# First scores of the second attention inside its value projection, its weight preparation in quarters; stick-breaking's first value slab fetched ahead of the key slab

## The chip, the cores and the metric

The kernel runs on one core of one Trainium2 chip. The metric is the device time of one execution in microseconds. The kernel before took 2044.36 us as the median of three runs (2042.57 to 2048.69). The execution from which the trace comes took 2052.48 us; all rows below come from that one.

## The reference, cut to what matters

Two transformer blocks run one after the other on one sequence of 512 tokens, width 1024, in float32. The first is feed-forward, a mixer, feed-forward. The second is retention followed by stick-breaking attention. Two places matter here.

```python
# block 1, the mixer: 12 heads in three dilation groups; one softmax over all three groups' keys comes out of the mixture
q, k, v = heads(u @ w_in)                      # u = rms_norm(h)
q, k = apply_partial_rope(q), apply_partial_rope(k)
s = einsum(q, k) * HEAD_DIM ** -0.5; s = where(allowed, s, -inf)   # per group
p = exp(s - max(s)); o = einsum(p, v) / sum(p); lse = max(s) + log(sum(p))
alpha = softmax(stack(lses)); y = sum(alpha * stack(outs))
# block 2, stick-breaking: 8 heads, keys and values from kv = rms_norm(h, kv_norm) @ w_kv
z = einsum(q, k) / sqrt(128)                   # q = (rms_norm(h, sb_norm_pre) @ sb_w_in)[:, :1024]
log_not = where(causal, log_sigmoid(-z), 0)
weights = exp(log_sigmoid(z) + reverse_cumsum(log_not) - log_not)
out = einsum(weights, v)
```

## The kernel before, in words

The order of the work is written out by hand, once per engine, with semaphores between the engines. Every weight comes as a slab of 128x2048 numbers (1 MB) into one of two slots (`raw`, `RING = 2`). ScalarE copies a slab to its rounded part `w_hi` (`prep`, L349) once the slot's former slab is used up, VectorE computes the rest `w_lo = raw - w_hi` (L728), and TensorE multiplies in three passes (high by high, low by high, high by low: L1339, L1340, L1341) into the banks of `acc` or `att` (four each). SyncE fetches slab n (`fetch`, L253) once slab n-2 is prepared. `prep` is called one slab ahead of its use, at fixed places in the order of ScalarE and VectorE.

The mixer has two attentions, `attend(0)` and `attend(1)`, of two head columns each. Each takes eight units (a token residue times a head). A unit k on TensorE is `scores(k)` (nine matmuls on 64 rows), `turn(k)` (six fp32 matmuls at L1499 that transpose the probabilities and scale them by `diag`) and the mix with the values (six matmuls at L1520). In the loop TensorE does `scores(k + 2)`, `turn(k + 1)`, mix k. On VectorE a unit is: scale and mask the scores (L888, L890), their maximum (L893), the low part of the transposed probabilities of unit k + 1 (L915, L917), a reciprocal (L908), and the sum of the mix (L932). On ScalarE: copy the transposed probabilities (L474, L476), exp (L452), `diag` (L458). Between units, `between()` prepares one whole slab: on ScalarE at k = 5, on VectorE at k = 6.

Ahead of each attention stands the value projection `values(x, strided, ...)`: four blocks of 24 matmuls, one per residue, whose stationary operand is every fourth token of `x`. In the second attention the last key rotation (`rotate_last`, L1443 and L1444) stands behind block 1, and the first two scores (`first_scores`) stand behind block 3, directly ahead of `attend(1)`. In the first attention the first scores stand one whole strided value projection ahead of `attend(0)`.

Stick-breaking begins in `sb_start`. TensorE makes the first keys from slab `sb_kq[0]` and the first values from slab `sb_v[0]`, interleaved over the input chunks, then eight fp32 matmuls for a mean (L1725, shown as 16), then the query, again from `sb_kq[0]`, then the turned norms (L1399). The third slab, `sb_g[0]`, goes into the slot of `sb_kq[0]`; its `prep` stands last in `sb_start` on both engines, behind `split_values` (L444 and L789). Then `sb_body` starts: four score matmul groups, then `pair()` with slab `sb_g[0]`, then the cumulative sums (L1686, L1687) that need `sp_lo`. For these VectorE goes through L1250, L1255, L1257, L1263 and L738, and ScalarE through L669, L671 and L354.

Of the kernel before, what the change touches and what calls it, by code (L numbers as in the profile page):

```python
# [30 lines left out]
SLAB = 16 * BLK  # L31
RING = 2
# [56 lines left out]
def block_kernel(nc, dram, out):  # L89
    with ExitStack() as ctx:  # L90
# [129 lines left out]
        w_ready = sem("w_ready")  # L220
        seg_done = sem("seg_done")
# [24 lines left out]
        def _(sp):  # L246
# [48 lines left out]
            for j in range(2):  # L295
                fetch(dram["ret_out"][RET_HEADS - 1, j])
            fetch(dram["sb_kq"][0])
            fetch(dram["sb_v"][0])
# [39 lines left out]
        def _(act):  # L338
# [3 lines left out]
            def prep(cols=SLAB):  # L342


                slot = n.k % RING
                act.wait_ge(raw_landed[slot], n.landed())
                if s.k:
                    act.wait_ge(seg_done, s.at())
                nc.scalar.activation(w_hi[:, slot, 0:cols], raw[:, slot, 0:cols], ACT.Copy).then_inc(w_hi_ready, 1)  # L349
                n.next()  # L350

# [118 lines left out]
            def attend(a, between=None):  # L470
# [10 lines left out]
                for k in range(UNITS):  # L481
                    if k == UNITS - 3 and between is not None:
                        between()
                    if k + 1 < UNITS:
                        stage(k + 1)
                    if k + 2 < UNITS:
                        exps(k + 2)
                        normalizer(k + 2)

# [29 lines left out]
            attend(0, prep)  # L519
# [5 lines left out]
            mix_values(2, 1)  # L525
            exps(1)
            normalizer(1)
            attend(1, prep)
# [125 lines left out]
            def sb_start():  # L654

                split_kq(0)
                std_of()
# [4 lines left out]
                prep()  # L662
# [56 lines left out]
        def _(dve):  # L719
            n, s, u, b = Count(), Count(), Count(), Count()  # L720
            fn, hi, step, sq, prob, mix, op, squared = (Count() for _ in range(8))
# [3 lines left out]
            def prep(cols=SLAB):  # L725
# [3 lines left out]
                n.next()  # L729

# [179 lines left out]
            def attend(a, between=None):  # L910
# [10 lines left out]
                for k in range(UNITS):  # L921
                    if k == UNITS - 2 and between is not None:
                        between()
# [4 lines left out]
                    if k + 2 < UNITS:  # L928
# [4 lines left out]
                                            ALU.add).then_inc(acc_free, 2)  # L933
                u.next(2 * UNITS)
# [57 lines left out]
            attend(0, prep)  # L992
# [6 lines left out]
            normalizer(0)  # L999
            mix_values(2, 1)  # L1000
            normalizer(1)
            attend(1, prep)
# [217 lines left out]
            def sb_start():  # L1220

                split_kq(0)
                rstd_of()
# [6 lines left out]
                prep()  # L1230
# [83 lines left out]
        def _(pe):  # L1314
# [237 lines left out]
            values(x, strided, {1: rotate_last, 3: first_scores})  # L1552
# [153 lines left out]
            def sb_start():  # L1706

                w, wv = slab(), slab()
# [156 lines left out]
```

## Time and profile before

| | |
|---|---|
| three timed runs, median | 2044.36 us |
| profiled execution, its time | 2052.48 us |
| its span, first to last instruction | 2050.7 us |
| TensorE matmul busy | 1978.7 us (96%) |
| VectorE busy | 1189.1 us (58%) |
| ScalarE busy | 700.0 us (34%) |
| mean granted TensorE clock | 0.979 of full |

TensorE is the busy engine nearly everywhere, so a time is found where TensorE stands idle or where its granted clock is below full. In the timeline each row is one instruction or a run of equal ones: start, duration, line, operation, and in square brackets the idle time before it with the instruction that ended it. Durations of matmuls overlap, so the step from one start to the next says what one costs.

### The profile page before, as it was taken

The numbers are of one execution on the slowest core, as the hardware profiler recorded it, in microseconds if no ns is written. First come the engines' busy times: TensorE is split into PE (matmuls) and PEld (weight loads), VectorE is DVE, ScalarE is ACT, GpSimd is POOL, SyncE is SP. The second block draws the span as 40 slices with busy tenths as digits, with TensorE's granted clock in tenths as the row PEclk, the third lists the DMA queues.
The fourth block names the chain that finished last, engine by engine and source line by source line (L and its number), as shares of the span: only waits on it lengthen the run. The fifth ranks groups of instructions, "written<-read, shape, count | busy, mean of one in ns | idle before, by whom it ended". The sixth has DMA issues, their size and how long they took to land.

```text
span 2050.7 us, 24191 instructions
## 1 busy us (share of the span) xinstructions
PE 1978.7 (96%) x9308; PEld 1668.2 (81%) x9308; DVE 1189.1 (58%) x1418; ACT 700.0 (34%) x744; POOL 11.3 (1%) x19
## 2 busy tenths in 40 slices
PE   7999999999999999999999999999997999999995
PEld 5888888889887788888888888888885788888884
DVE  5343355675545566434455658584859665555557
ACT  4222232334224333222232233232324544444443
POOL 0000000000000000000000000000000000000000
PEclk9999999999969999999999999999998999999998
DMA  4222223320202222222223322221212122222211
GB/s 174 92 92 102 83 85 99 121 78 11 78 0 78 92 103 97 89 101 102 84 80 108 129 82 84 81 95 69 102 62 82 42 83 70 75 81 82 82 62 41
DMA packets 27413, 171.77 MB, mean 84 GB/s; under 512 B 3184, under 2 KB 3200, under 8 KB 10464
## 3 DMA queue, kind: packets, MB, share of 16 engines
q1 hardware_dynamic: 25344, 165.95, 23.0%
q0 software_dynamic: 864, 2.99, 0.4%
q10 hardware_dynamic: 1152, 2.10, 0.3%
q8 instruction: 37, 0.61, 0.1%
q14 instruction: 16, 0.13, 0.0%
HBM read 168.93 MB, written 2.10 MB: 83 GB/s over the span
## 4 chain that ended last, share of the span: by engine, by line
PE 90%; DVE 6%; ACT 2%; issue 1%; DMA 0%; DVEq 0%; ACTq 0%; POOLq 0%
PE acc L1339 27%; PE acc L1340 26%; PE acc L1341 26%; PE att L1339 2%; PE att L1341 2%; PE att L1340 2%; PE acc L1499 1%; DVE w_lo L728 1%; ACT w_hi L349 1%; DVE rstd L769 1%; PE acc L1520 1%; PE att L1687 1%; PE att L1686 1%; DVE tmp L1187 0%; PE att L1725 0%
## 5 line engine op out<-in xcount | busy, mean ns | idle before, releaser
L1339 PE MATMUL acc<-x_hi,w_hi 128*128 128x512 f32 x1408 | 555.5, 395 | 20.0 <-DVE w_lo L728 17.9
L1340 PE MATMUL acc<-x_lo,w_hi 128*128 128x512 f32 x1408 | 549.9, 391 | 0.0
L1341 PE MATMUL acc<-x_hi,w_lo 128*128 128x512 f32 x1408 | 549.9, 391 | 0.0
L728 DVE TENSOR_TENSOR w_lo<-raw,w_hi 128x2048 fp32r<-128x2048 f32 (+1 forms) x168 | 383.0, 2280 | 140.0 <-ACT w_hi L349 135.7
L349 ACT ACTIVATE w_hi<-raw 128x2048 fp32r<-128x2048 f32 (+1 forms) x168 | 318.8, 1898 | 106.4 <-PE acc L1341 103.0
L1339 PEld LDWEIGHTS acc<-x_hi,w_hi 128*128 128x128 f32 x1408 | 265.4, 188 | 78.6 <-DVE w_lo L728 18.0
L1340 PEld LDWEIGHTS acc<-x_lo,w_hi 128*128 128x128 f32 x1408 | 265.6, 189 | 56.9 <-issue 2.4
L1341 PEld LDWEIGHTS acc<-x_hi,w_lo 128*128 128x128 f32 x1408 | 265.5, 189 | 55.9
L1339 PE MATMUL acc<-g_hi,w_hi 128*128 128x512 f32 x352 | 136.9, 389 | 0.0
L1340 PE MATMUL acc<-g_lo,w_hi 128*128 128x512 f32 x352 | 136.9, 389 | 0.0
L1341 PE MATMUL acc<-g_hi,w_lo 128*128 128x512 f32 x352 | 136.9, 389 | 0.0
L382 ACT ACTIVATE tmp<-tmp 128x512 f32<-128x512 f32 x44 | 27.8, 632 | 293.3 <-DVE tmp L801 293.3
L801 DVE TENSOR_TENSOR tmp<-acc,rstd 128x512 f32<-128x512 f32 x44 | 30.4, 691 | 159.3 <-PE acc L1341 159.2
L1339 PE MATMUL acc<-w_hi,x_hi 128*128 128x512 f32 (+1 forms) x224 | 84.6, 378 | 1.1 <-DVE w_lo L728 1.1
L1340 PE MATMUL acc<-w_lo,x_hi 128*128 128x512 f32 (+1 forms) x224 | 84.5, 377 | 0.0
L1341 PE MATMUL acc<-w_hi,x_lo 128*128 128x512 f32 (+1 forms) x224 | 84.4, 377 | 0.0
L1341 PEld LDWEIGHTS acc<-g_hi,w_lo 128*128 128x128 f32 x352 | 66.1, 188 | 13.8
L1340 PEld LDWEIGHTS acc<-g_lo,w_hi 128*128 128x128 f32 x352 | 66.1, 188 | 13.7
L1339 PEld LDWEIGHTS acc<-g_hi,w_hi 128*128 128x128 f32 x352 | 66.1, 188 | 13.6
L1339 PE MATMUL acc<-w_hi,kv_hi 128*128 128x256 f32 x224 | 63.7, 284 | 0.0
L1340 PE MATMUL acc<-w_lo,kv_hi 128*128 128x256 f32 x224 | 63.4, 283 | 0.0
L1341 PE MATMUL acc<-w_hi,kv_lo 128*128 128x256 f32 x224 | 63.4, 283 | 0.0
(277 smaller groups left out, 2922.8 us busy)
## 6 DMA issues: line engine op xcount, KB each, us to landing
raw<-in_ffn_up SPq DMA_DIRECT2D x44, 1024.0 KB, 4.7
raw<-in_ret_head SPq DMA_DIRECT2D x24, 1024.0 KB, 4.7
raw<-in_ffn_down SPq DMA_DIRECT2D x32, 704.0 KB, 4.0
raw<-in_mix_gate SPq DMA_DIRECT2D x8, 1024.0 KB, 4.8
raw<-in_ret_out SPq DMA_DIRECT2D x8, 1024.0 KB, 4.7
raw<-in_sb_kq SPq DMA_DIRECT2D x8, 1024.0 KB, 4.7
raw<-in_sb_v SPq DMA_DIRECT2D x8, 1024.0 KB, 4.7
raw<-in_sb_g SPq DMA_DIRECT2D x8, 1024.0 KB, 4.7
```

The source lines that it names most:

```text
L349: nc.scalar.activation(w_hi[:, slot, 0:cols], raw[:, slot, 0:cols], ACT.Copy).then_inc(w_hi_ready, 1)
L382: nc.scalar.activation(t(j), t(j), ACT.Silu).then_inc(fn_ready, 1)
L728: tt(w_lo[:, slot, 0:cols], raw[:, slot, 0:cols], w_hi[:, slot, 0:cols].bitcast(F32), ALU.subtract).then_inc(w_ready, 1)
L769: nc.vector.reciprocal(dst[:], t(std)).then_inc(att_free, 1 + skip)
L801: tt(t(j), acc[:, u.k % BANKS, :], rstd[:], ALU.mult).then_inc(acc_free, 1)
L1339: mm(dst, still[0], move[0], start=first, stop=False)
L1340: mm(dst, still[0], move[1], start=False, stop=False)
L1341: return mm(dst, still[1], move[0], start=False, stop=last)
L1499: last = mm(dst[i // TB][:, P * (i % TB):P * (i % TB) + P], tmp[:, at:at + P], diag[:, k % 2, :], start=True, stop=True)
L1520: last = mm(dst, va[:, k_blk, value_slot(g, head)].rearrange("p s d -> p (s d)"), turned_probs[:, k % 2, i].rearrange("p s q -> p (s q)"), ...
L1686: mm(dst[:, P * (k - m):TRI[m]], still[:], sp_hi[:, cols], start=k == m, stop=False)
L1687: ins = mm(dst[:, P * (k - m):TRI[m]], still[:], sp_lo[:, cols], start=False, stop=k == TB - 1)
```

## The change

Three edits, and what goes with them.

1. In the second attention TensorE's rotation moves behind block 0 of the value projection, and the first two scores move behind block 1, ahead of blocks 2 and 3. ScalarE and VectorE do `exps`/`normalizer` of both units before they take over values 2 and 3.
2. In both attentions the slab is prepared in four parts of 512 columns, at the end of the iterations k = 1 to 4, on ScalarE behind `normalizer(k + 2)` and on VectorE behind the sum of mix k. A new semaphore `w_part_ready` passes the first three parts on.
3. SyncE fetches `sb_v[0]` ahead of `sb_kq[0]`; TensorE takes the two in that order. So `sb_g[0]` goes into the slot of `sb_v[0]`, and its `prep` moves on ScalarE and VectorE from the end of `sb_start` to directly behind `split_kq(0)`.

```diff
+PARTS = 4
+PART = SLAB // PARTS
@@ sync
+            fetch(dram["sb_v"][0])
             fetch(dram["sb_kq"][0])
-            fetch(dram["sb_v"][0])
             fetch(dram["sb_g"][0])
@@ scalar
+            def prep_part(i):
+                slot, cols = n.k % RING, slice(PART * i, PART * (i + 1))
+                if i == 0:
+                    act.wait_ge(raw_landed[slot], n.landed())
+                    act.wait_ge(seg_done, s.at())
+                nc.scalar.activation(w_hi[:, slot, cols], raw[:, slot, cols], ACT.Copy).then_inc(
+                    w_hi_ready if i == PARTS - 1 else w_part_ready, 1)
+                if i == PARTS - 1:
+                    n.next()
@@ scalar, attend
                 for k in range(UNITS):
-                    if k == UNITS - 3 and between is not None:
-                        between()
                     if k + 1 < UNITS:
                         stage(k + 1)
                     if k + 2 < UNITS:
                         exps(k + 2)
                         normalizer(k + 2)
+                    if 1 <= k <= PARTS:
+                        prep_part(k - 1)
@@ scalar, second attention
             exps(0)
             normalizer(0)
-            mix_values(2, 1)
             exps(1)
             normalizer(1)
-            attend(1, prep)
+            mix_values(2, 1)
+            attend(1)
@@ scalar, sb_start
                 split_kq(0)
+                prep(seg=2)
                 std_of()
...
-                prep()
@@ vector
+            def prep_part(i):
+                slot, cols = n.k % RING, slice(PART * i, PART * (i + 1))
+                if i < PARTS - 1:
+                    dve.wait_ge(w_part_ready, part.next())
+                else:
+                    dve.wait_ge(w_hi_ready, n.at(1))
+                ins = tt(w_lo[:, slot, cols], raw[:, slot, cols], w_hi[:, slot, cols].bitcast(F32), ALU.subtract)
...
@@ vector, attend
-                    if k == UNITS - 2 and between is not None:
-                        between()
...
                     nc.vector.tensor_reduce(o_unit[:, k, :], ...).then_inc(acc_free, 2)
+                    if 1 <= k <= PARTS:
+                        prep_part(k - 1)
@@ tensor
-            values(x, strided, {1: rotate_last, 3: first_scores})
+            values(x, strided, {0: rotate_last, 1: first_scores})
@@ tensor, sb_start
-                w, wv = slab(), slab()
+                wv, w = slab(), slab()
```

VectorE inside `attend(0)`, one iteration of the loop (k = 1) before, from the scaled scores to the next ones:

```order
L888 SCALAR_TENSOR_TENSOR tmp<-att,band 128x512 [waits att_full]
L890 SCALAR_TENSOR_TENSOR tmp<-att,classes 128x256
L893 TENSOR_REDUCE neg_max<-tmp 128x1 [waits att_free]
L915 TENSOR_TENSOR stage<-acc,stage 128x4x128 [waits hi_ready]
L917 TENSOR_TENSOR stage<-acc,stage 128x2x128 [waits hi_ready]
L908 RECIPROCAL rden<-den 128x1 [waits prob_ready]
L932 TENSOR_REDUCE tmp<-acc 128x128 [waits mixed]
L888 SCALAR_TENSOR_TENSOR tmp<-att,band 128x512 [waits att_full]
```

The same iteration in the changed kernel, whose line numbers are higher by 24 to 26:

```order
L914 SCALAR_TENSOR_TENSOR tmp<-att,band 128x512 [waits att_full]
L916 SCALAR_TENSOR_TENSOR tmp<-att,classes 128x256
L919 TENSOR_REDUCE neg_max<-tmp 128x1 [waits att_free]
L941 TENSOR_TENSOR stage<-acc,stage 128x4x128 [waits hi_ready]
L943 TENSOR_TENSOR stage<-acc,stage 128x2x128 [waits hi_ready]
L934 RECIPROCAL rden<-den 128x1 [waits prob_ready]
L956 TENSOR_REDUCE tmp<-acc 128x128 [waits mixed]
L752 TENSOR_TENSOR w_lo<-raw,w_hi 128x512 [waits w_part_ready]
L914 SCALAR_TENSOR_TENSOR tmp<-att,band 128x512 [waits att_full]
```

A quarter of the slab now stands between two units, and it waits for ScalarE's quarter of the same iteration.

TensorE at the end of value block 1 of the second attention before (the blocks are L1339 to L1341 on `x`, the rotation is L1443 and L1444):

```order
L1341 MATMUL acc<-w_hi,x_lo 128x256
L1443 MATMUL att<-stage,rot_r 128x512
L1444 MATMUL att<-stage,rot_r 128x512
L1339 MATMUL acc<-w_hi,x_hi 128x256
L1340 MATMUL acc<-w_lo,x_hi 128x256
```

The same place in the changed kernel:

```order
L1367 MATMUL acc<-w_hi,x_lo 128x256
L1365 MATMUL att<-qk_hi 128x512
L1366 MATMUL att<-qk_lo,qk_hi 128x512
L1367 MATMUL att<-qk_hi,qk_lo 128x512
L1365 MATMUL att<-qk_hi 128x128
```

The scores (`att<-qk`) now stand where the rotation stood, and blocks 2 and 3 follow them; the rotation stands one block earlier.

VectorE from the first key split of stick-breaking to its first scaled scores before (L728 is the preparation of slab `sb_g[0]`):

```order
L738 TENSOR_TENSOR skq_lo<-acc,skq_hi 128x512 [waits hi_ready]
L769 RECIPROCAL rstd<-tmp 128x512 [waits fn_ready]
L738 TENSOR_TENSOR skq_lo<-acc,skq_hi 128x512 [waits hi_ready,att_free]
L782 COPY r_tok<-att 128x4 [waits att_full]
L1227 TENSOR_SCALAR z_scale<-r_tok 128x4 [waits att_free]
L789 SCALAR_TENSOR_TENSOR sv_lo<-acc,r_tok,sv_hi 128x256 [waits hi_ready,dve_step]
L789 SCALAR_TENSOR_TENSOR sv_lo<-acc,r_tok,sv_hi 128x256
L789 SCALAR_TENSOR_TENSOR sv_lo<-acc,r_tok,sv_hi 128x256 [waits hi_ready]
L789 SCALAR_TENSOR_TENSOR sv_lo<-acc,r_tok,sv_hi 128x256
L728 TENSOR_TENSOR w_lo<-raw,w_hi 128x2048 [waits w_hi_ready]
L1250 SCALAR_TENSOR_TENSOR tmp<-att,z_scale,rstd 128x512 [waits att_full,op_ready]
```

The same stretch in the changed kernel:

```order
L764 TENSOR_TENSOR skq_lo<-acc,skq_hi 128x512 [waits hi_ready]
L742 TENSOR_TENSOR w_lo<-raw,w_hi 128x2048 [waits w_hi_ready]
L795 RECIPROCAL rstd<-tmp 128x512 [waits fn_ready]
L764 TENSOR_TENSOR skq_lo<-acc,skq_hi 128x512 [waits hi_ready,att_free]
L808 COPY r_tok<-att 128x4 [waits att_full]
L1254 TENSOR_SCALAR z_scale<-r_tok 128x4 [waits att_free]
L815 SCALAR_TENSOR_TENSOR sv_lo<-acc,r_tok,sv_hi 128x256 [waits hi_ready,dve_step]
L815 SCALAR_TENSOR_TENSOR sv_lo<-acc,r_tok,sv_hi 128x256
L815 SCALAR_TENSOR_TENSOR sv_lo<-acc,r_tok,sv_hi 128x256 [waits hi_ready]
L815 SCALAR_TENSOR_TENSOR sv_lo<-acc,r_tok,sv_hi 128x256
L1276 SCALAR_TENSOR_TENSOR tmp<-att,z_scale,rstd 128x512 [waits att_full,op_ready]
```

The preparation of `sb_g[0]` moved from behind the value splits to ahead of the reciprocal.

## Rows read from the trace of the kernel before

**Rows 1.** Page, part 2: granted TensorE clock in 40 slices of 51.3 us.
```profile
PEclk9999999999969999999999999999998999999998
```

**Rows 2.** Timeline, TensorE, first attention: start, us, line, operation, [idle before].
```profile
481.60 1.50 PE L1499 MATMUL acc<-tmp 128*128 128x128 f32 x12
...
505.68 0.63 PE L1339 MATMUL att<-qk_hi 64*128 64x512 f32 x1
...
507.96 1.60 PE L1499 MATMUL acc<-tmp 128*128 128x128 f32 x12
...
511.83 1.60 PE L1499 MATMUL acc<-tmp 128*128 128x128 f32 x12 [1.55 <-ACT tmp L458]
...
514.87 0.98 PE L1520 MATMUL acc<-stage,va 128*128 128x256 f32 x6 [0.73 <-DVE stage L917]
```

**Rows 3.** Timeline, TensorE, second attention.
```profile
564.72 0.28 PE L1339 MATMUL acc<-w_hi,x_hi 128*128 128x256 f32 x1
...
579.09 0.41 PE L1341 MATMUL att<-qk_hi,qk_lo 64*128 64x128 f32 x1
582.85 2.93 PE L1499 MATMUL acc<-tmp 128*128 128x128 f32 x12 [3.35 <-ACT tmp L458]
...
618.62 0.62 PE L1339 MATMUL att<-qk_hi 64*128 64x512 f32 x1
...
627.81 0.98 PE L1520 MATMUL acc<-stage,va 128*128 128x256 f32 x6 [0.73 <-DVE stage L917]
```

**Rows 4.** Stretches: length, busy and instructions per engine, granted clock, DMA share, GB/s.
```profile
40.00:60.00 20.00, 20.00 (x90) 16.57 (x89) 7.73 (x8) 5.51 (x5) 0.00 (x0) 1.00 0.34 123
...
459.00:460.00 1.00, 1.00 (x6) 1.00 (x5) 0.97 (x2) 0.00 (x0) 0.00 (x0) 0.50 1.00 418
462.00:463.00 1.00, 1.00 (x6) 1.00 (x6) 0.02 (x1) 0.95 (x2) 0.00 (x0) 1.00 0.63 262
584.00:588.00 4.00, 4.00 (x17) 3.51 (x15) 1.66 (x5) 1.71 (x5) 0.00 (x0) 0.50 0.00 0
```

**Rows 5.** Timeline, TensorE, start of stick-breaking.
```profile
1620.63 0.27 PE L1341 MATMUL att<-skq_hi,skq_lo 128*128 128x128 f32 x1
1624.56 0.50 PE L1339 MATMUL acc<-x_hi,w_hi 128*128 128x512 f32 x1 [3.66 <-DVE w_lo L728]
...
1637.19 0.41 PE L1686 MATMUL att<-sp_hi,tri_r 128*128 128x512 f32 x1
```

**Rows 6.** Timeline, VectorE, start of stick-breaking.
```profile
1619.75 1.66 DVE L789 SCALAR_TENSOR_TENSOR sv_lo<-acc,r_tok,sv_hi 128x256 fp32r<-128x256 f32 x4 [0.77 <-ACT sv_hi L444]
...
1624.42 1.92 DVE L1250 SCALAR_TENSOR_TENSOR tmp<-att,z_scale,rstd 128x512 f32<-128x512 f32 x4
...
1635.56 1.49 DVE L738 TENSOR_TENSOR sp_lo<-tmp,sp_hi 128x1280 fp32r<-128x1280 f32 x1 [1.34 <-ACT sp_hi L354]
```

**Rows 7.** Timeline, VectorE: first scaled scores of the second attention.
```profile
578.37 0.69 DVE L888 SCALAR_TENSOR_TENSOR tmp<-att,band 128x512 f32<-128x512 f32 x1 [9.73 <-PE att L1341]
```

**Rows 8.** Timeline, ScalarE: second `diag` of the second attention, and start of stick-breaking.
```profile
584.66 0.40 ACT L458 ACTIVATE tmp<-ident,rden 128x128 f32<-128x128 f32 x1 [0.23 <-DVE rden L908]
...
1611.84 0.69 ACT L363 ACTIVATE tmp<-att,eps 128x512 f32<-128x512 f32 x1 [7.70 <-PE att L1725]
```

**Rows 9.** Timeline, VectorE, small slab preparation and two units of the first attention.
```profile
457.50 0.68 DVE L728 TENSOR_TENSOR w_lo<-raw,w_hi 128x512 fp32r<-128x512 f32 x1
458.10 0.68 DVE L888 SCALAR_TENSOR_TENSOR tmp<-att,band 128x512 f32<-128x512 f32 x1
...
503.54 0.69 DVE L888 SCALAR_TENSOR_TENSOR tmp<-att,band 128x512 f32<-128x512 f32 x1 [0.92 <-PE att L1341]
...
508.07 0.69 DVE L888 SCALAR_TENSOR_TENSOR tmp<-att,band 128x512 f32<-128x512 f32 x1 [0.92 <-PE att L1341]
```

**Rows 10.** Timeline, ScalarE: the small slab preparation, and the whole one in the first attention.
```profile
455.02 0.64 ACT L349 ACTIVATE w_hi<-raw 128x512 fp32r<-128x512 f32 x1
...
507.15 1.89 ACT L349 ACTIVATE w_hi<-raw 128x2048 fp32r<-128x2048 f32 x1
```

More of the change, by code:

```diff
@@ L220, in block_kernel @@
         w_ready = sem("w_ready")
+        w_part_ready = sem("w_part_ready")
         seg_done = sem("seg_done")
@@ L340, in _, with prep @@
             val, turn, inv = Count(), Count(), Count()
-            def prep(cols=SLAB):
+            def prep(cols=SLAB, seg=0):
                 slot = n.k % RING
@@ L347, in prep @@
                 if s.k:
-                    act.wait_ge(seg_done, s.at())
+                    act.wait_ge(seg_done, s.at(seg))
                 nc.scalar.activation(w_hi[:, slot, 0:cols], raw[:, slot, 0:cols], ACT.Copy).then_inc(w_hi_ready, 1)
                 n.next()
+            def prep_part(i):
[7 more added lines that the diff above has]
+                    n.next()
             def split_val(dst, src):
@@ L468, in gather, with attend @@
                                      ACT.Copy).then_inc(hi_ready, 1)
-            def attend(a, between=None):
+            def attend(a):
                 def stage(k):
@@ L518, in _ @@
             mix_values(1, 1)
-            attend(0, prep)
+            attend(0)
             qk(True)
@@ L720, in _ @@
             n, s, u, b = Count(), Count(), Count(), Count()
-            fn, hi, step, sq, prob, mix, op, squared = (Count() for _ in range(8))
+            fn, hi, step, sq, prob, mix, op, squared, part = (Count() for _ in range(9))
             tt = nc.vector.tensor_tensor
@@ L729, in prep @@
                 n.next()
+            def prep_part(i):
[5 more added lines that the diff above has]
+                ins = tt(w_lo[:, slot, cols], raw[:, slot, cols], w_hi[:, slot, cols].bitcast(F32), ALU.subtract)
+                if i == PARTS - 1:
+                    ins.then_inc(w_ready, 1)
+                    n.next()
             def link(ins):
@@ L908, in normalizer, with attend @@
                 nc.vector.reciprocal(rden[:, k:k + 1], den[:, k:k + 1]).then_inc(rden_ready, 1)
-            def attend(a, between=None):
+            def attend(a):
                 def low_probs(k):
@@ L991, in _ @@
             mix_values(1, 1)
-            attend(0, prep)
+            attend(0)
             qk(True)
@@ L999, in _ @@
             normalizer(0)
+            normalizer(1)
             mix_values(2, 1)
-            normalizer(1)
-            attend(1, prep)
+            attend(1)
             gather(1)
@@ L1222, in sb_start @@
                 split_kq(0)
+                prep()
                 rstd_of()
@@ L1229, in sb_start @@
                     split_values(lambda k: sv_lo[:, k:k + 1, :], lambda k: sv_hi[:, k:k + 1, :], o, 0, whole_row)
-                prep()
             def sb_out(first, last):
```

## The prediction

> **What bounds the kernel now.** I read the page first. TensorE is busy nearly everywhere, and its granted clock has one deep hole: slices 12 and 13 of 40 read 9 and 6 [rows 1], and the timeline shows that the hole is the second attention. The timeline of TensorE there and the same place in the first attention are the two stretches to lay side by side. Both do the same instructions. In the first, `turn(0)` starts at 481.60, `scores(7)` at 505.68 and the last mix at 514.87 [rows 2]. In the second the first scores end at 579.50, TensorE stands idle for 3.35 us until `diag` is there, `turn(0)` starts at 582.85, `scores(7)` at 618.62, the last mix at 627.81 [rows 3]. From `turn(0)` to `scores(7)` that is 24.08 us against 35.77, and from there to the last mix 9.19 in both. The granted clock says why: 0.50, which is 1.2 GHz, from 584 to 588 [rows 4], and the twelve matmuls of a turn take 2.93 us where they take 1.50 in the first [rows 2, 3].
>
> Then the timeline at the start of stick-breaking. TensorE ends its scores at 1620.90 and starts the pair with slab `sb_g[0]` at 1624.56, after 3.66 us of idle time ended by `w_lo` [rows 5]. VectorE starts its scaled scores at 1624.42, behind that same `w_lo` [rows 6].
>
> **Edit 1, the scores inside the value projection.** No matmul is added or taken out. Blocks 2 and 3 now stand between the scores and `turn(0)`. Block 2 starts at 564.72 and the scores end at 579.50 [rows 3]; two score groups take at most 2.3 us each (505.68 to 507.96) [rows 2], so the two blocks give at least 10.2 us of cover. What must fit under them is the chain from the first scaled scores to the second `diag`. It started at 578.37 [rows 7] and ended at 585.06 [rows 8], so 6.7 us; it started 1.1 us before the end of the scores, so it ends 5.6 us behind that, and over 4 us are spare. VectorE now takes over values 0 and 1 in front of it, and four such takeovers take 1.66 us [rows 6]. If the cover fell away, at most the 3.35 us would come back. The takeover of values 2 and 3 slides behind the start of `turn(0)`, exactly where the first attention has it, and there it holds nobody up. Gain: 3.35 us of idle time.
>
> The larger part is the clock. It fell around the idle time and stayed at 1.2 GHz for most of the attention. Entered at 2.4 GHz, the second attention should take what the first takes: 35.77 - 24.08 = 11.69 us less.
>
> One rule has to be held against that. The rows show a fall with no idle time at all: at 459 TensorE was fully busy at 0.50, just behind the first attention's first scores, and at 462 it was back at 1.00, both times inside the strided value blocks [rows 4]. The changed kernel puts just these scores ahead of just such blocks, so I expect such a fall here too. It costs nothing there: six matmuls stand in a microsecond at either level [rows 4]. The Trainium skill, "TensorE: Matmul & The Clock Gate", Part 1, says that "the default state is throttled, and activity releases the throttle", and puts the low state down to idleness. By that rule closing the gap is enough; by the row at 459 it isn't, and the entry into the attention must find the clock raised again. The rule alone gives the sum below, the row without the recovery at 462 gives rival A.
>
> **Edit 2, the preparation in quarters.** It removes one ScalarE copy (1.89 us) and one VectorE subtraction per attention and adds four of each. Two ends. On the good side, the last mix waits 0.73 us for `stage` behind the whole subtraction [rows 2, 3]; a good part of that wait is the ordinary chain turn, copy, subtract, so I book 0.2 us. On the bad side stands a loop through two engines. VectorE starts the scaled scores of a unit at 503.54 [rows 9]; ScalarE is through with `diag` and free at 507.15 [rows 10]: 3.61 us. Behind it now come ScalarE's quarter, 0.64 us [rows 10], and VectorE's quarter, which waits for it and holds up the next scaled scores by 0.60 us (457.50 to 458.10) [rows 9]. The sum is 4.85 us, and a unit on TensorE has 508.07 - 503.54 = 4.53 [rows 9]. So each of four iterations makes VectorE 0.32 us later, 1.28 us in all. The slack: `turn(6)` starts 4.42 us behind its scaled scores (503.54 to 507.96), while `turn(7)`, which waits for nothing else, starts 3.76 behind (508.07 to 511.83) [rows 2, 9]. So 0.66 us are hidden at first, but `turn(7)` has no slack, and gets the whole 1.28 us. Queued behind the waiting quarter on VectorE are the scaled scores, for which ScalarE's exp and then TensorE's turn wait. Net per attention 1.28 - 0.2 = 1.1 us lost, 2.2 for both. Bounds: 0.7 gained each (the whole wait) to 1.3 lost each. I take the lost end, since its terms are rows. The slab itself was not waited for here, so having it earlier brings nothing; SyncE's next fetch comes about 10 us earlier, into an idle queue.
>
> **Edit 3, the value slab first.** `sb_g[0]`'s preparation moves into a hole: ScalarE was idle for 7.70 us before 1611.84 [rows 8], and VectorE's next instruction waits for that copy. Into this fit 1.9 us and then at most four times 0.60. Both slabs are needed for the first matmul either way, so their exchange costs nothing. VectorE's scaled scores then start at 1619.75 + 1.66 = 1621.41 in place of 1624.42: 3.01 us earlier [rows 6]. The pair could start at 1620.90, 3.66 us earlier, and at full clock. What is late next is `sp_lo`: it ended at 1637.05 and the cumulative sums started at 1637.19, without idle time [rows 5, 6]. So the gain is the smaller one, 3.0 us, if ScalarE's part of the chain shifts with it, and the pair, 48 matmuls where 90 go in 20 us [rows 4], takes 10.7 us and ends at 1631.6, leaving some 2.6 us idle before the sums at about 1634.2. Bounds: 0 to 3.7 us. SyncE's fetch of `sb_v[1]` comes some 15 us earlier, with nothing behind it.
>
> **The sum**, against the profiled execution: 2052.48 - 3.35 - 11.69 + 2.2 - 3.0 = 2036.6 us. The median is 8.1 us below that execution, and this is the weakest place of the forecast. If the difference is in every profiled run, the median of the changed kernel is 2044.4 - 15.8 = 2028.5. If it is clock that the profiled run lost and the timed runs did not, it is 2036.6. The three timed runs lie 6.1 us apart, about half of the 11.7, which looks like clock. I take the middle, 2032.5. The Trainium skill, same page and part, says of the cold start that "it's run-variable"; the spread agrees with it, but no row here shows a second execution.
>
> **Rivals.**
> A. The clock is low on entry all the same, because it falls behind the moved scores and isn't raised before `turn(0)`. Then only the idle time goes, the quarters are hidden in the slow units, and the sum is 2044.4 - 3.35 - 3.0 + 1.1 = 2039.1. For it: the fall at 459. Against it: at 462 it had been raised, under the same blocks, which go on for 10 us or more here.
> B. The new gaps cost clock. `turn(7)` now waits 1.55 + 1.28 = 2.8 us in both attentions [rows 2], and stick-breaking gets the 2.6 us. What a short fall costs before dense matmuls is in the rows: 1624.56 to 1637.19 is 12.6 us [rows 5], 1.9 more than 10.7. Three times that: 2032.5 + 5.7 = 2038.2. For it: lengths of gaps near 3.35. Against it: the gap of 1.55 us fell nowhere.
> C. Slower: the quarters open waits inside the first attention's units, the clock falls there before `turn(1)`, and both attentions run at 1.2 GHz. The first then pays the 11.7 us that only the second paid, the second gets only its 3.35 back, the quarters cost nothing at that pace: 2044.4 + 11.7 - 3.35 - 3.0 = 2049.7. It decides only if the fall comes in the first units; the first wait that I compute comes at `turn(6)`, which speaks against it.
> D. Nothing moves, since the timed runs never lost the clock that the trace lost and the quarters eat the rest: 2044.
>
> **Chances.** Forecast 0.69, A 0.11, B 0.12, C 0.05, D 0.03. A change of 0.3% (6.1 us) is about what a measurement can tell, so faster means below 2038.2. Of the forecast nearly all, of A four tenths and of B half lie below: 0.80 faster. The same 0.14, slower 0.06. The range must hold 2028.5 with the quarters hidden and the whole 3.7 us (2025) and reach through B and A: 2025 to 2041.
>
> **What would show it.** In the changed kernel's trace: `turn(0)` of the second attention directly behind value block 3, a turn there in about 1.5 us, 24 us from it to `scores(7)`, and the clock at 1.00; `turn(7)` in the first attention 31.5 us behind `turn(0)` instead of 30.2, with its wait grown from 1.55 to 2.8; in stick-breaking no wait of the pair, and one of about 2.6 us ahead of the sums, for `sp_lo`. I am wrong if the second attention reads 0.50 again, or if `turn(7)` is not later.

## The result: 8 to 10 us faster, and a forecast that was 8 us too low

The changed kernel takes 2040.51 us (median of 16 runs, 2038.75 to 2042.11), the kernel before 2048.45 us (16 runs, 2042.14 to 2058.50). The ratio is 0.9959, interval 0.9946 to 0.9972. On a second occasion it was 2039.97 against 2049.89 us, ratio 0.9955 (0.9937 to 0.9974). The time lies in the forecast range, near its upper end, and the kernel is faster by more than 0.3%. The value of 2032.5 us was 8.0 us too low. Three executions in the whole record stand far outside the others (2494.82 and 8305.98 us of the kernel before, 5971.66 us of `e7_tails_filled`); they are left out of the ranges below, and without them the medians beside them would be 0.1 to 0.3 us lower.

The profiled execution of the changed kernel took 2041.25 us (span 2039.4), that of before 2052.48 (span 2050.7). The deep hole in the granted clock is gone. The page of the changed kernel, part 2, answers to [rows 1]:

```profile
PEclk9999999999999999999999999999998999999998
```

The timeline of TensorE in the changed kernel answers to [rows 2] and [rows 3]. The first three rows are of the first attention, the others of the second: `turn(0)`, the first row of `scores(7)`, `turn(7)` and the last mix, then the gather behind it.

```profile
484.50 1.50 PE L1525 MATMUL acc<-tmp 128*128 128x128 f32 x12
...
511.19 2.12 PE L1525 MATMUL acc<-tmp 128*128 128x128 f32 x12 [0.26 <-ACT tmp L472]
516.05 2.92 PE L1525 MATMUL acc<-tmp 128*128 128x128 f32 x12 [1.46 <-ACT tmp L472]
...
584.61 1.50 PE L1525 MATMUL acc<-tmp 128*128 128x128 f32 x12
...
608.68 0.63 PE L1365 MATMUL att<-qk_hi 64*128 64x512 f32 x1
...
616.15 1.60 PE L1525 MATMUL acc<-tmp 128*128 128x128 f32 x12 [2.54 <-ACT tmp L472]
...
619.04 0.98 PE L1546 MATMUL acc<-stage,va 128*128 128x256 f32 x6 [0.58 <-DVE stage L943]
620.61 1.98 PE L1500 MATMUL att<-tmp,fold 128*128 128x512 f32 x4 [0.59 <-DVE tmp L956]
```

`turn(0)` of the second attention has no wait in brackets any more, and from it to `scores(7)` are 24.07 us (584.61 to 608.68) in place of 35.77. ScalarE had both `diag` long ready:

```profile
576.22 0.40 ACT L472 ACTIVATE tmp<-ident,rden 128x128 f32<-128x128 f32 x1 [0.95 <-DVE rden L934]
...
577.77 0.40 ACT L472 ACTIVATE tmp<-ident,rden 128x128 f32<-128x128 f32 x1 [0.23 <-DVE rden L934]
```

`turn(0)` waits only for the first of them, which was ready at 576.62, 8.0 us before TensorE starts at 584.61. Even the second, which `turn(1)` reads at 588.32, was there 6.4 us before `turn(0)`. In the first attention `turn(7)` starts 31.55 us behind `turn(0)` (484.50 to 516.05), 1.32 later than before. It takes 2.92 us, the time of a turn at 1.2 GHz; before it took 1.60 [rows 2].

The granted clock of these stretches in the changed kernel (length, busy and instructions of PE, PEld, DVE, ACT and POOL, then PEclk, DMA share, GB/s), to be laid beside [rows 4]:

```profile
508.00:511.00 3.00, 2.93 (x15) 2.62 (x13) 2.80 (x7) 1.70 (x5) 0.00 (x0) 1.00 0.00 0
511.00:512.00 1.00, 0.81 (x7) 0.82 (x8) 0.36 (x2) 0.65 (x2) 0.00 (x0) 1.00 0.00 0
512.00:515.00 3.00, 2.59 (x14) 2.29 (x12) 2.96 (x6) 1.65 (x3) 0.00 (x0) 0.52 0.41 134
515.00:518.00 3.00, 1.95 (x9) 1.96 (x10) 0.73 (x3) 0.76 (x3) 0.00 (x0) 0.50 0.51 216
...
574.00:576.00 2.00, 2.00 (x10) 2.00 (x10) 1.97 (x4) 1.03 (x2) 0.00 (x0) 0.50 0.00 0
584.00:588.00 4.00, 4.00 (x25) 3.88 (x24) 1.80 (x4) 1.71 (x4) 0.00 (x0) 1.00 0.00 0
```

There is a fall behind the moved scores (574 to 576), and it is over before the attention begins (584 to 588 reads 1.00 where [rows 4] read 0.50). There is also a new one at the end of the first attention, low for 6.8 us. In the second profiled execution of the same kernel, `after_again`, it is 3.4 us long, and the first attention takes 34.44 us there and not 35.40.

At the start of stick-breaking the timeline of TensorE answers to [rows 5], and that of VectorE to [rows 6]:

```profile
1609.17 0.50 PE L1365 MATMUL att<-skq_hi 128*128 128x512 f32 x1 [0.70 <-DVE skq_lo L764]
...
1624.41 0.51 PE L1712 MATMUL att<-sp_hi,tri_r 128*128 128x512 f32 x1 [2.15 <-DVE sp_lo L764]
...
1628.80 0.45 PE L1365 MATMUL acc<-kv_hi,w_hi 128*128 128x512 f32 x1
```

```profile
1610.16 1.66 DVE L815 SCALAR_TENSOR_TENSOR sv_lo<-acc,r_tok,sv_hi 128x256 fp32r<-128x256 f32 x4 [0.77 <-ACT sv_hi L458]
1611.74 1.92 DVE L1276 SCALAR_TENSOR_TENSOR tmp<-att,z_scale,rstd 128x512 f32<-128x512 f32 x4
...
1622.87 1.49 DVE L764 TENSOR_TENSOR sp_lo<-tmp,sp_hi 128x1280 fp32r<-128x1280 f32 x1 [1.34 <-ACT sp_hi L368]
```

The pair no longer waits (no row of it has brackets), VectorE's scaled scores follow the splits at once, and the sums wait 2.15 us for `sp_lo`. Then the sums run slowly: their windows show the clock down exactly there.

```profile
1621.00:1624.00 3.00, 1.26 (x6) 0.72 (x4) 1.66 (x2) 2.42 (x2) 0.00 (x0) 1.00 0.50 208
1624.00:1628.00 4.00, 3.58 (x15) 3.44 (x15) 2.24 (x4) 2.64 (x4) 0.00 (x0) 0.60 0.00 0
```

The whole difference between the two profiled executions, from the starts of the same rows in both timelines:

| stretch | before | after | difference | forecast |
|---|---|---|---|---|
| start to first `turn(0)` | 481.60 | 484.50 | +2.90 | 0 |
| first attention, `turn(0)` to last mix | 33.27 | 35.40 | +2.13 | +1.1 |
| last mix to second `turn(0)` | 67.98 | 64.71 | -3.27 | -3.35 |
| second attention, `turn(0)` to gather | 46.52 | 36.00 | -10.52 | -10.6 |
| gather to first scores of stick-breaking | 989.39 | 988.56 | -0.83 | 0 |
| these scores to the sums | 18.43 | 15.24 | -3.19 | -3.0 |
| sums to the next key slab | 2.74 | 4.39 | +1.65 | 0 |
| from there to the end | 410.77 | 410.60 | -0.17 | 0 |

The differences add up to the 11.3 us between the spans. These are two single executions; the kernel before varies by 16 us from run to run, so its row for the second attention stands for its slower runs.

### The profile page after: what moved, and what is told of

Its sections match the earlier page's. It is cut to its first block, busy times and chain, and to the rows that moved or that the text cites. A ratio compares the mean times of both kernels' runs of the same rounds, so it can differ in the third digit from the quotient of the medians.

```text
span 2039.4 us, 24203 instructions
## 1 busy us (share of the span) xinstructions
PE 1968.8 (97%) x9308; PEld 1660.7 (81%) x9308; DVE 1189.2 (58%) x1424; ACT 701.1 (34%) x750; POOL 11.3 (1%) x19
## 4 chain that ended last, share of the span: by engine, by line
PE 88%; DVE 7%; ACT 3%; issue 1%; DMA 0%; DVEq 0%; ACTq 0%
PE acc L1365 26%; PE acc L1367 26%; PE acc L1366 26%; PE att L1365 2%; PE att L1367 2%; PE att L1366 2%; ACT w_hi L352 1%; DVE w_lo L742 1%; DVE rstd L795 1%; PE att L1713 1%; PE att L1712 1%; ACT tmp L466 1%; DVE neg_max L919 0%; PE acc L1525 0%; DMA h<-in_x 0%
## 5 line engine op out<-in xcount | busy, mean ns | idle before, releaser
L742 DVE TENSOR_TENSOR w_lo<-raw,w_hi 128x2048 fp32r<-128x2048 f32 (+1 forms) x166 | 378.4, 2280 | 141.3 <-ACT w_hi L352 137.2
```

The source lines that it names most:

```text
L742: tt(w_lo[:, slot, 0:cols], raw[:, slot, 0:cols], w_hi[:, slot, 0:cols].bitcast(F32), ALU.subtract).then_inc(w_ready, 1)
```

## The experiments

In all of them the pattern of the clock is read from the granted clock in windows of 1 us. "Low for 34.1 us" means the sum of the time at 1.2 GHz in one such stretch.

### Each edit alone, and two together

The scores alone, `e1_scores_only`:

```
-            values(x, strided, {1: rotate_last, 3: first_scores})
+            values(x, strided, {0: rotate_last, 1: first_scores})
```

(and the order of `mix_values`, `exps(1)` and `normalizer(1)` that goes with it).

> The kernel before with edit 1 alone (rotation and first scores inside the value projection; whole slab preparation as before). Theory (the wait ahead of the second attention costs the clock of that attention): the 3.35 us of idle time go, turn(0) to scores(7) takes 24.1 us as in the first attention at a granted clock of 1.00, and since runs of the kernel before lose different amounts of clock there, the median falls by 3.35 plus 4 to 8 us, that is by 7 to 11 us, and the runs lie closer together than those of before. Rival (only the idle time counts, the clock is lost somewhere in the attention anyway): 3.4 us less and the spread stays.

Measured: 2038.82 us (2037.20 to 2040.77) against 2049.95 of the kernel before, ratio 0.9941 (0.9920 to 0.9962).

The quarters alone, `e2_quarters_only`: both `prep_part` functions and their calls, the scores and the slab as before.

> The kernel before with edit 2 alone (slab preparation of both attentions in quarters). Theory (the loop VectorE scores, ScalarE exp and diag, ScalarE quarter, VectorE quarter is 0.3 us longer than a unit): turn(6) and turn(7) of the first attention come 0.3 and 1.3 us later, the longer wait ahead of turn(7) can cost the clock there, and the time rises by 1 to 3 us (the second attention, at half clock, hides its quarters). Rival (quarters fit between the units, the whole slab was in the way of the last mix): 0.2 to 0.7 us less per attention.

Measured: 2046.97 us (2045.73 to 2047.96), ratio 0.9986 (0.9973 to 0.9998).

The slab of stick-breaking alone, `e3_slab_only`:

```
-                w, wv = slab(), slab()
+                wv, w = slab(), slab()
```

(with the exchanged fetches and the two moved `prep` calls).

> The kernel before with edit 3 alone (first value slab ahead of the key slab, its successor prepared in the hole). Theory: the pair starts 3.7 us earlier, the cumulative sums 3.0 us earlier, a wait of 2.2 us for sp_lo opens ahead of them; 2 to 3.2 us less, according to the clock after that wait. Rival (the new wait costs a clock stretch as long as the old one and cancels the gain): 0 to 1.5 us less.

Measured: 2049.88 us (2042.26 to 2055.32), ratio 0.9991 (0.9973 to 1.0009). That is 0.1 us less than before; the 2 to 3.2 us of the theory did not come, and the number is that of the rival.

Scores and slab without the quarters, `e4_no_quarters`:

> The changed kernel without edit 2 (edits 1 and 3 alone). Theory: turn(7) waits 1.55 us in both attentions, no clock is lost at the end of the first, and the time is 2 to 4 us below that of the changed kernel, 2036.5 to 2038.5. Rival (the quarters are free): the same as the changed kernel, 2040.5.

Measured: 2037.78 us (2036.96 to 2038.30), ratio 0.9936 (0.9915 to 0.9957).

What follows: edit 1 brings 11.1 us, more than the whole change. Edit 3 on top of it brings 1.0 us (2038.82 to 2037.78). The quarters take back 2.7 us (2037.78 to 2040.51, on two occasions; 2.2 us against the 2039.97 of the other occasion). That the quarters alone are not slower but 3 us faster than before (2046.97 against 2049.95) does not fit this sum. The timeline of that kernel shows the idle time ahead of the second attention whole, and a slow `turn(0)`, but the next turn (591.34, 1.60 us) is fast again, and its windows show why:

```profile
586.03 2.93 PE L1525 MATMUL acc<-tmp 128*128 128x128 f32 x12 [3.35 <-ACT tmp L472]
```

```profile
582.00:590.00 8.00, 4.65 (x19) 4.18 (x20) 5.58 (x12) 4.34 (x10) 0.00 (x0) 0.57 0.00 0
590.00:594.00 4.00, 4.00 (x26) 3.76 (x26) 2.52 (x5) 1.38 (x3) 0.00 (x0) 1.00 0.02 4
```

Here the clock was low for 6.8 us, about half of it the gap itself. In the kernel before it was low for 34.1 us around the same gap. These windows are of the kernel before:

```profile
590.00:600.00 10.00, 10.00 (x41) 9.16 (x41) 5.44 (x12) 4.19 (x9) 0.00 (x0) 0.50 0.00 0
600.00:610.00 10.00, 10.00 (x38) 9.00 (x38) 4.27 (x10) 2.70 (x6) 0.00 (x0) 0.50 0.00 0
610.00:614.00 4.00, 4.00 (x19) 3.78 (x19) 2.85 (x7) 1.89 (x4) 0.00 (x0) 0.50 0.00 0
615.00:619.00 4.00, 4.00 (x26) 3.76 (x26) 2.49 (x4) 1.35 (x3) 0.00 (x0) 1.00 0.00 0
```

So the length of the slow stretch is not fixed by the gap. Two kernels test that.

### Is it the gap, and what sets how long the clock stays down?

`e6_gap_filled` is the kernel before with 14 matmuls in the gap, whose result goes into a free bank and is read by nobody:

```
+            pe.wait_ge(acc_free, u.at(1))
+            for i in range(14):
+                mm(acc[:, u.k % BANKS, :], x_hi[:, i % DC, 0:P], x_hi[:, i % DC, :], start=True, stop=True)
             attend(1)
```

> The kernel before with 14 matmuls of 512 columns (3.2 us) into a free bank between its first scores and turn(0) of the second attention; their result is overwritten, nothing is left out. Order and waits stay. Theory (the idle 3.35 us make the clock fall): the attention runs at 1.00, turn(0) to scores(7) takes 24.1 us, the runs lie close together, and the median falls by 6 to 9 us although no wait is shorter. Rival (the clock falls because of the 64-row scores ahead of the attention, idle or not): the attention still reads 0.50 in part and the median stays near that of before.

Measured: 2043.04 us (2039.63 to 2045.19), ratio 0.9972 (0.9957 to 0.9987). The timeline shows the filler where the idle time was, and turns of 1.60 us behind it:

```profile
581.48 3.47 PE L1556 MATMUL acc<-x_hi 128*128 128x512 f32 x14
584.90 1.60 PE L1500 MATMUL acc<-tmp 128*128 128x128 f32 x12
```

```profile
582.00:586.00 4.00, 4.00 (x22) 3.17 (x22) 2.77 (x6) 2.58 (x6) 0.00 (x0) 1.00 0.00 0
586.00:590.00 4.00, 4.00 (x25) 3.77 (x24) 2.81 (x8) 1.74 (x6) 0.00 (x0) 1.00 0.02 4
```

`turn(0)` starts at the same distance from the scores as before, so nothing but the clock has changed, and the kernel is about 6.9 us faster (2049.92 to 2043.04). So the loss of clock in the second attention hangs on the idle gap: the scores ahead of it are the same, and in the profiled execution with the gap filled the clock does not fall behind them. Value blocks in the gap, as in edit 1, are better still, since they also give back the gap itself: from the filled gap to edit 1 alone are another 4.2 us (2043.04 to 2038.82), 3.3 of them idle time. The Trainium skill, "TensorE: Matmul & The Clock Gate", Part 1, puts the low state down to idleness; this run agrees with it. The fall at 459 us, with TensorE fully busy [rows 4], does not.

`e8_shift` leaves the gap alone and puts six such matmuls, 1.36 us of work, ahead of the second attention's queries and keys, 65 us before the gap:

```
             units_done = u.k + BANKS
+            pe.wait_ge(acc_free, u.at(1))
+            for i in range(6):
+                mm(acc[:, u.k % BANKS, :], x_hi[:, i % DC, 0:P], x_hi[:, i % DC, :], start=True, stop=True)
             qk(True)
```

> The kernel before with 6 matmuls of 512 columns (1.36 us) between attend(0) and the next projection; everything behind comes 1.36 us later, nothing else moves. Quarters alone made the runs of the kernel before lie close together (2045.7 to 2048.0) though the gap ahead of the second attention was still there. Theory (how long the clock stays low in the second attention depends on when, counted from the start of the kernel, the gap falls, and the quarters only moved it by 1.2 us): with the shift the slow runs over 2050 vanish too, the runs lie within 3 us, and the median is at or below that of before minus 1 us in spite of 1.36 us more work. Rival (the quarters themselves helped the clock recover): the runs spread over 10 us as those of before, and the median rises by 1.4 us.

Measured: 2043.60 us (2041.81 to 2048.47), ratio 0.9972 (0.9954 to 0.9989). With more work and the gap untouched it is about 6.3 us faster than before. All 12 runs have a mean granted clock of 0.985 to 0.988, which only 16 of 66 runs of the kernel before reach; one of the 12 (2048.47 us) lies outside the 3 us that the theory gave them. The timeline and the windows show the gap and a short fall:

```profile
586.11 2.93 PE L1500 MATMUL acc<-tmp 128*128 128x128 f32 x12 [3.35 <-ACT tmp L459]
```

```profile
582.00:590.00 8.00, 4.65 (x19) 4.21 (x19) 5.66 (x12) 4.34 (x10) 0.00 (x0) 0.57 0.00 0
590.00:594.00 4.00, 4.00 (x26) 3.76 (x26) 2.49 (x4) 1.35 (x3) 0.00 (x0) 1.00 0.01 4
```

The two profiled executions alone would not show this: that of `e8_shift` has the gap 3.26 us later than that of before, of which only 1.36 are the filler, and the rest lies ahead of the first attention. When the clock falls differs too. The first row is of the kernel before, the second of `e8_shift`:

```profile
580.00:581.00 1.00, 0.00 (x0) 0.00 (x0) 1.00 (x3) 0.59 (x1) 0.00 (x0) 0.87 0.00 0
582.00:583.00 1.00, 0.76 (x4) 0.58 (x3) 0.97 (x3) 0.00 (x0) 0.00 (x0) 0.84 0.00 0
```

A mean of 0.87 over one microsecond puts the fall before at 580.7, which is 1.2 us into the idle time. The 0.84 puts that of `e8_shift` at 582.7, and its idle time begins at 582.76, so this fall comes with the end of the scores and can't be put down to the gap behind them. In `e2_quarters_only` it is the same (0.85 in that microsecond, idle from 582.68).

What follows: filling the gap takes the low stretch away, and moving the same gap in time changes how long the clock stays down (6.8 or 34.1 us in the profiled executions). By what rule the place decides isn't shown. The spread of the kernel before goes with the clock. Over 66 of its timed runs, those taken beside the experiments, the time follows the mean granted clock of the run:

| mean clock of the run | runs | time, us | median |
|---|---|---|---|
| 0.984 to 0.988 | 24 | 2041.86 to 2047.90 | 2045.4 |
| 0.980 to 0.983 | 17 | 2048.40 to 2052.91 | 2049.8 |
| 0.976 to 0.979 | 25 | 2052.62 to 2058.47 | 2054.6 |

The changed kernel's 16 runs span 3.4 us. That these differences of clock all lie in the second attention isn't shown, since timed runs have no trace; the kernels without the gap, `e1`, `e4` and `e6`, span 1.3 to 5.6 us.

### The quarters

`e5_vector_later` is the changed kernel with VectorE's quarter one iteration later, so that ScalarE has long finished it:

```
-                    if 1 <= k <= PARTS:
-                        prep_part(k - 1)
+                    if 2 <= k <= PARTS + 1:
+                        prep_part(k - 2)
```

> The changed kernel with VectorE's quarter one iteration later than ScalarE's (k = 2 to 5), so that it no longer waits for the quarter of its own iteration. Theory (the loop of two engines is 0.3 us too long because VectorE waits there): without that wait the loop is 3.19 + 0.34 + 0.60 us, under the 4.53 of a unit; turn(7) of the first attention starts 30.2 to 30.3 us behind turn(0) instead of 31.55, the clock is not lost there, and the time is 2 to 3 us below the changed kernel, near 2038. Rival (it is the amount of work on the two engines, not the wait): turn(7) stays at 31.5 and the time at 2040.5.

Measured: 2036.82 us (2035.20 to 2038.55), ratio 0.9942 (0.9922 to 0.9962). The timeline, first attention, `turn(6)`, `turn(7)` and the last mix:

```profile
510.83 1.60 PE L1525 MATMUL acc<-tmp 128*128 128x128 f32 x12
514.70 1.60 PE L1525 MATMUL acc<-tmp 128*128 128x128 f32 x12 [1.55 <-ACT tmp L472]
...
517.60 0.98 PE L1546 MATMUL acc<-stage,va 128*128 128x256 f32 x6 [0.59 <-DVE stage L943]
```

`turn(7)` is back at 30.23 us behind `turn(0)`, and the clock no longer falls there. The loop between the engines is seen directly in the changed kernel: VectorE's quarters, each followed by the scaled scores that it holds up, come every 4.86 us, for which 4.85 had been worked out.

```profile
501.97 0.69 DVE L752 TENSOR_TENSOR w_lo<-raw,w_hi 128x512 fp32r<-128x512 f32 x1 [0.64 <-ACT w_hi L361]
502.57 0.68 DVE L914 SCALAR_TENSOR_TENSOR tmp<-att,band 128x512 f32<-128x512 f32 x1
...
506.83 0.69 DVE L752 TENSOR_TENSOR w_lo<-raw,w_hi 128x512 fp32r<-128x512 f32 x1 [0.64 <-ACT w_hi L361]
507.44 0.68 DVE L914 SCALAR_TENSOR_TENSOR tmp<-att,band 128x512 f32<-128x512 f32 x1
```

To be sure of the lead, both kernels ran again on one chip. `e5_again`:

> The kernel with all three edits and the quarters at k = 2 to 5 once more, on the same chip as the two beside it, as what they are compared with. Theory: 2036.8 us within 1 us, the last turn of the first attention 30.2 us behind its first. Rival: its lead over the changed kernel (2040.5) was between chips, and it is at 2039 to 2041 us.

Measured: 2036.63 us (2035.15 to 2038.01), ratio 0.9933 (0.9907 to 0.9958). `after_again`:

> The changed kernel itself, on the same chip as the three beside it. Theory: 2040.5 us within 1 us, 3 to 4 us slower than with the quarters at k = 2 to 5, of which 1.3 us are the late last turn of the first attention and 0.8 us the clock behind it, and the like of 1.2 us in the second. Rival: no difference between the two on one chip.

Measured: 2039.97 us (2038.63 to 2042.27). The lead of 3.3 us stands on one chip too, with no run of the one reaching into the range of the other, and `e5_vector_later` beats the changed kernel. It is 1.0 to 1.2 us faster than the one without quarters (2037.78, another occasion), a difference that I don't call shown.

`e7_tails_filled` is the changed kernel with ten filler matmuls ahead of `turn(7)` in both attentions, against the fall at the end of the first:

```
+                    if k == UNITS - 1:
+                        keep_busy(10)
                     pe.wait_ge(diag_ready, prob.next())
```

> The changed kernel with 10 matmuls of 512 columns (2.3 us) into a free bank ahead of turn(7) of both attentions, where TensorE waits 2.5 to 2.8 us. Theory (the longer wait is what costs the clock at the end of the first attention): the clock stays at 1.00 there, and the time falls by 0.8 to 1.5 us. Rival (no clock is lost through the wait): the same time as the changed kernel.

Measured: 2041.04 us (2039.71 to 2042.71), ratio 0.9959 (0.9944 to 0.9975), no faster than the changed kernel. Its windows and the filler's row in its timeline show the reason: the clock is down from 511 to 514, and the filler starts at 514.16. The filler also holds `turn(7)` up: it starts 32.74 us behind `turn(0)` in place of 31.55, so the time alone would not have decided between theory and rival.

```profile
511.00:514.00 3.00, 3.00 (x18) 3.00 (x17) 2.77 (x5) 1.30 (x4) 0.00 (x0) 0.55 0.36 85
```

```profile
514.16 2.74 PE L1520 MATMUL att<-x_hi 128*128 128x512 f32 x10
```

My theory for this place, that the wait ahead of `turn(7)` makes the clock fall, has fallen: the fall comes ahead of the wait, in this kernel and in the changed one (512 to 515). It came with every kernel that has the quarters in the same iteration (the changed kernel twice, `e2`, `e7`) and with none of the others. What in these kernels triggers it stays open. All four have a wait of some 0.25 us ahead of `turn(6)` just before it, which the others don't have, but the changed kernel has the same wait in the second attention (611.29) and no fall there. `after_again` has one there, at 610.0, for 3.4 us.

### Stick-breaking

`e11_sums_filled` is `e5` with nine filler matmuls where TensorE waits for `sp_lo`:

```
+                if first:
+                    pe.wait_ge(att_free, b.at(1))
+                    for i in range(9):
+                        mm(att[:, b.k % BANKS, :], x_hi[:, i % DC, 0:P], x_hi[:, i % DC, :], start=True, stop=True)
                 pe.wait_ge(op_ready, op.next())
```

> The kernel with all three edits and the VectorE quarter brought back two key blocks sooner (the parts at k = 2 to 5), plus 9 matmuls of 128x512 into a free accumulator bank ahead of the cumulative sums of stick-breaking, where TensorE waited 2.15 us for sp_lo. Theory: that idle stretch is what makes the clock fall to 1.2 GHz during the sums, so with it filled the sums to the next scores take 2.7 us and not 4.4, and the kernel is 1.0 to 1.6 us shorter than the same one without the filler (near 2035.3 us). Rival: the fall comes from something else, or only moves, and the time stays within 0.5 us of the one without the filler (2036.8).

Measured: 2036.99 us (2035.55 to 2037.82), against 2036.63 without the filler on the same chip. The place itself behaved as the theory has it. Filler, first sum and next key slab in its timeline:

```profile
1617.62 2.20 PE L1708 MATMUL att<-x_hi 128*128 128x512 f32 x9
1619.94 0.50 PE L1716 MATMUL att<-sp_hi,tri_r 128*128 128x512 f32 x1
...
1622.75 0.44 PE L1365 MATMUL acc<-kv_hi,w_hi 128*128 128x512 f32 x1
```

The sums take 2.81 us (1619.94 to 1622.75), where the kernel without the filler takes 4.38. But the time did not follow, as the rival had it. In the profiled execution the gain is given back near the end: from the last product with the values to the final norm this kernel takes 22.70 us, and `e5_again` 21.19. First the filled kernel, then `e5_again`:

```profile
1994.37 0.50 PE L1365 MATMUL att<-sp_hi,sv_hi 128*128 128x512 f32 x1 [2.18 <-DVE sp_lo L764]
2002.14 0.50 PE L1365 MATMUL acc<-so_hi,w_hi 128*128 128x512 f32 x1 [2.17 <-DVE so_lo L764]
2017.07 1.12 PE L1403 MATMUL att<-ssq,mean_d 128*128 128x512 f32 x2 [2.18 <-DVE ssq L790]
```

```profile
1996.76 0.50 PE L1365 MATMUL att<-sp_hi,sv_hi 128*128 128x512 f32 x1 [2.18 <-DVE sp_lo L764]
2002.98 0.53 PE L1365 MATMUL acc<-so_hi,w_hi 128*128 128x512 f32 x1 [2.17 <-DVE so_lo L764]
2017.95 1.13 PE L1403 MATMUL att<-ssq,mean_d 128*128 128x512 f32 x2 [2.18 <-DVE ssq L790]
```

Between the first two rows lie 7.77 us in the filled kernel and 6.22 in the other. Both have the same wait of 2.18 us, but only in the filled one does the clock fall behind it (a stretch of 3.4 us from 1995).

`e12_no_slab` is `e5` without edit 3.

> The same kernel (moved scores, quarters at k = 2 to 5) without the moved value slab of stick-breaking. Theory: edit 3 is worth 3.2 us of work brought forward less 1.65 us for the low clock in the sums, so this kernel is 1.0 to 1.7 us slower than the one with it (near 2038.2 us). Rival: the full 3.0 us of the prediction, so 2039.8 us.

Measured: 2037.80 us (2035.36 to 2038.64), 1.2 us more than with edit 3, as the theory had it. Its profiled execution shows no fall between 1616 and 2021 us, and the stretch from the product with the values to the final norm takes 19.54 us. From the first scores of stick-breaking to the final norm the profiled executions give:

| kernel | scores to sums | sums | tail | scores to final norm |
|---|---|---|---|---|
| before | 18.43 | 2.74 | 21.15 | 413.94 |
| edit 3 alone | 15.25 | 4.00 | 22.71 | 413.97 |
| edit 1 | 19.70 | 2.72 | 21.14 | 415.18 |
| edits 1 and 3 | 15.24 | 4.38 | 21.02 | 412.26 |
| `e5_again` | 15.25 | 4.38 | 21.19 | 412.44 |
| `e12_no_slab` | 18.35 | 2.80 | 19.54 | 412.31 |
| `e11_sums_filled` | 15.26 | 2.81 | 22.70 | 412.39 |

The tail is the stretch that the rows above mark, from the product with the values to the final norm. It takes 19.5, 21.1 or 22.7 us, with none, one or two short falls of the clock in it. Edit 3 brings the sums 3.1 to 4.5 us forward, and up to all of it is lost again to falls that come at other places: in the sums and in the tail. In the medians it is worth 1.0 (`e1` to `e4`) and 1.2 us (`e12_no_slab` to `e5_again`), with ranges of runs that overlap; alone (before to `e3`) it is worth 0.1. None of the three is clear of noise, and between `e12_no_slab` and `e5_again` the table shows none of it.

## Why the prediction was right, and where it was wrong

**Edit 1, right in mechanism, its size only for one execution.** The idle time went (3.27 of the 3.35 us), the second attention became 10.52 us shorter with the quarters in it (10.6 forecast), the fall behind the moved scores came and cost nothing, and the clock was up again at `turn(0)`. Rival A is out by the window at 584. The filled gap shows the cause by experiment. But 11.69 us is what one of the slower executions lost; by the medians edit 1 as a whole is worth 11.1 us and not 15.0. The chain was read up to the second `diag`, while `turn(0)` waits only for the first; that erred on the safe side.

**Edit 2, right in mechanism.** The loop of 4.85 us, the 1.28 us at `turn(7)` (measured 1.32) and their cause are confirmed by `e5`. The wait ahead of `turn(7)` was forecast at 2.8 us. In the second attention it is 2.54, since `turn(6)` already takes 0.25 of it; in the first it is 1.46, since `turn(6)` and its mix also ran slowly. Not in the sum: the fall at the end of the first attention, 0.8 us of the 2.13 in this execution and nearly nothing in `after_again`. Forecast 2.2 us, measured 2.2 or 2.7 by the medians (`e4_no_quarters` against the two occasions of the changed kernel), and 3.3 against the same quarters one iteration later.

**Edit 3, the step that failed.** "So the gain is the smaller one, 3.0 us": the place moved by 3.19 us, the wait for `sp_lo` came (2.15 for 2.6), and then the sums themselves took 1.65 us more at the low clock. The term was 0.1 to 1.2 us in the medians, not 3.0. This was the mechanism of rival B, which named this gap and was given 0.12. Of B's three places two cost something, 0.8 and 1.65 us, and that is 2.5 of its 5.7 us; the 0.8 did not come through the wait that B named, as `e7` shows.

**The sum and the median, the step that failed most.** The sum against the profiled execution was 2036.6 us, and the profiled execution of the changed kernel took 2041.25. Of the 4.65 us between them 2.9 are the start, where the first slab came 1.2 us later (first matmul at 15.38 in place of 14.22 us) and the clock around 395 us was low for 6.8 in place of 3.4 us. This part is not of the change: the same stretch, with the same instructions, took 481.6 to 485.2 us in the profiled executions of all the kernels. The rest is the 1.65 and 0.8 us, less the 0.83 us between the gather and stick-breaking, and some remainders. From 2036.6 the forecast then went down by another 4.1 us: "The median is 8.1 us below that execution ... I take the middle." Three runs had been a lucky sample. With the 66 runs the median of before is 2049.8 us, 2.6 below its profiled execution, and for the changed kernel the two differ by 0.7 us. Of the two readings that the text offered, clock that the profiled run lost and the timed ones did not was the nearer one, and going by it the value would have been 2036.6. It is not quite right either: 25 of the 66 runs lost as much clock as the profiled one. That the measured time lies in the range is in part luck: 0.5 us more and it would have been outside. By the bar that the text set, below 2038.2, 2040.51 is not faster; that bar stood on the three runs, and against the 2048.45 of 16 runs the kernel is.

**Rivals C and D** are out: the first attention keeps its clock until 512 us, and the kernel is faster by an interval that excludes no change.

## What to carry to other kernels

Judge a gap of TensorE by the work that stands behind it too: here a gap of 3.35 us cost 3.35 us of idle time and, through the clock, another 7 us in the median. Filling it with work that is due anyway gives back both, with useless matmuls the second part. When work is cut into parts for two engines in turn, let the second engine take its part an iteration later than the first gives it out; written in the same iteration the parts cost 2.2 to 2.7 us here, one iteration later nothing that could be measured. And where a kernel's runs spread by 16 us, read the granted clock of each run before a difference between the profiled and the timed runs goes into a forecast.

## What the hardware showed that I had not expected

- A slow stretch of the clock around one and the same gap lasted 6.8 us, half of it idle, or 34.1 us, with TensorE fully busy in all but 2.1 of them. Six matmuls of extra work, 1.36 us, 65 us ahead of the gap made the kernel 6.3 us faster.
- The clock also fell where TensorE had been busy for 3.74 of the 4 us before (508 to 512 in the changed kernel), and it did not fall behind a wait of 2.54 us (616 in the second attention). The same wait of 2.18 us near the end of stick-breaking was followed by a fall in one kernel and by none in another.
- A gain of 1.57 us at the sums was gone at the end of the program, though the stretch between the two places took 371.62 us in both profiled executions. Small gains at the gaps of this kernel did not add up.
